# First attention of a three-part transformer kernel: the query root on GpSimd, a negated minimum for the softmax, an earlier exp table, reordered last additions

## The reference

```python
q = rmsnorm_2(q.reshape(B, S, A_HEADS, A_HEAD_DIM), q_gain)
k = rmsnorm_2(k.reshape(B, S, A_KV_HEADS, A_HEAD_DIM), k_gain)
...
scores = jnp.einsum('bnqkgd,bnskd->bnkgqs', q, kb).astype(jnp.float32) * scale   # scale = 1/8
bias = rel_bias[t5_bucket(dist)]
scores = scores + bias
scores = jnp.where(valid[None, :, None, None], scores, NEG)
m = jnp.maximum(jnp.max(scores, axis=-1, keepdims=True), sink)
p = jnp.exp(scores - m)
denom = jnp.sum(p, axis=-1, keepdims=True) + jnp.exp(sink - m)
probs = (p / denom).astype(v.dtype)
o = jnp.einsum('bnkgqs,bnskd->bnqkgd', probs, vb)
return o.reshape(B, S, A_HEADS * A_HEAD_DIM) @ w_out
```

## Time and profile before

| what | value |
|---|---|
| median of 3 runs (lowest, highest) | 2815.04 us (2812.4, 2815.44) |
| the profiled execution's own time | 2825.3 us |
| its span in the trace | 2824.1 us |
| PE busy | 2717.6 us (96%) |
| DVE busy | 1470.3 us (52%) |
| ACT busy | 974.7 us (35%) |
| POOL busy | 313.2 us (11%) |
| mean granted TensorE clock | 0.976 |

### The profile page before, as it was taken

One profiled execution on the slowest core, in us unless ns is written; L12 is line 12 of the kernel. 1 busy time (PEld: TensorE's weight loads), 2 busy tenths in 40 slices (PEclk: granted clock), 3 DMA queues, 4 the chain that ended last, 5 costly groups with the idle time before them and its releaser, 6 DMA issues.

```text
span 2824.1 us, 32255 instructions
## 1 busy us (share of the span) xinstructions
PE 2717.6 (96%) x13207; PEld 2278.7 (81%) x13207; DVE 1470.3 (52%) x2347; ACT 974.7 (35%) x1601; POOL 313.2 (11%) x381
## 2 busy tenths in 40 slices
PE   6899999999998999998999999999999888999999
PEld 5788788888786888888878888888888778888887
DVE  4635546665657545556665343544434466544433
ACT  3334333333353212234453222322223466432221
POOL 2000000000021000003340000000000467400000
PEclk9999999999999999998999999999999889999999
DMA  4322233623132287746223333232322100132331
GB/s 137 103 92 75 75 105 128 196 79 109 55 115 75 90 104 90 105 84 120 76 65 105 105 98 96 90 105 91 98 94 84 38 31 31 60 119 90 95 96 64
DMA packets 281195, 258.99 MB, mean 92 GB/s; under 512 B 40517, under 2 KB 276056, under 8 KB 281048
## 3 DMA queue, kind: packets, MB, share of 16 engines
q1 hardware_dynamic: 281047, 256.93, 33.1%
HBM read 242.23 MB, written 14.68 MB: 91 GB/s over the span
## 4 chain that ended last, share of the span: by engine, by line
PE 84%; DVE 9%; ACT 4%; issue 1%; SPq 1%; POOL 1%; DMA 1%; DVEq 0%; ACTq 0%; POOLq 0%
PE bank L1058 27%; PE bank L1059 26%; PE bank L1060 26%; DVE Wl L1730 1%; PE bank L1201 1%; PE bank L1069 1%; ACT Wh L1395 1%; SPq L2421 1%; PE bank L1343 1%; DVE Pl L1718 1%; DVE TMP L1923 1%; DVE TMP L1920 1%; DVE TMP L1799 0%; ACT TMP L1508 0%; DMA RAW<-in_a_w_in 0%
## 5 line engine op out<-in xcount | busy, mean ns | idle before, releaser
L1058 PE MATMUL bank<-Hh,Wl 128*128 128x512 f32 x2144 | 845.9, 395 | 15.1 <-DVE Hl L1746 15.1
L1059 PE MATMUL bank<-Hl,Wh 128*128 128x512 f32 x2144 | 838.7, 391 | 0.0
L1060 PE MATMUL bank<-Hh,Wh 128*128 128x512 f32 x2144 | 838.5, 391 | 0.0
L1395 ACT ACTIVATE Wh<-RAW 128x1024 fp32r<-128x1024 f32 (+2 forms) x454 | 441.0, 1023 | 440.6 <-PE bank L1060 378.3
L1730 DVE TENSOR_TENSOR Wl<-RAW,Wh 128x1024 fp32r<-128x1024 f32 (+2 forms) x420 | 492.7, 1216 | 172.2 <-ACT Wh L1395 171.7
L1058 PEld LDWEIGHTS bank<-Hh,Wl 128*128 128x128 f32 x2144 | 404.7, 189 | 103.9 <-issue 8.2
L1058 PE MATMUL bank<-Ph,Wl 128*128 128x512 f32 x1200 | 474.5, 395 | 13.2 <-DVE Pl L1812 3.5
L1060 PEld LDWEIGHTS bank<-Hh,Wh 128*128 128x128 f32 x2144 | 404.5, 189 | 86.3
L1059 PEld LDWEIGHTS bank<-Hl,Wh 128*128 128x128 f32 x2144 | 404.7, 189 | 84.9 <-issue 1.7
L1059 PE MATMUL bank<-Pl,Wh 128*128 128x512 f32 x1200 | 470.6, 392 | 0.0
L1060 PE MATMUL bank<-Ph,Wh 128*128 128x512 f32 x1200 | 470.4, 392 | 0.0
(11 more groups left out here) (296 smaller groups left out, 2506.4 us busy)
## 6 DMA issues: line engine op xcount, KB each, us to landing
RAW<-in_ffn_wg SPq DMA_DIRECT2D x44, 1024.0 KB, 5.3
RAW<-in_ffn_wu SPq DMA_DIRECT2D x44, 1024.0 KB, 5.3
RAW<-in_ffn_wd SPq DMA_DIRECT2D x32, 1024.0 KB, 5.2
RAW<-in_w_up SPq DMA_DIRECT2D x22, 1024.0 KB, 5.1
RAW<-in_w_in SPq DMA_DIRECT2D x20, 1024.0 KB, 5.1
RAW<-in_ffn_wd SPq DMA_DIRECT2D x16, 768.0 KB, 4.4
bias_scratch<-M SPq DMA_DIRECT2D x16, 512.0 KB, 8.0
RAW<-in_w_down SPq DMA_DIRECT2D x8, 1024.0 KB, 5.9
```

Source lines behind the costliest of these rows:

```text
L1058: mm(o, ll, rh, start=start, stop=False)
L1059: mm(o, lh, rl, start=False, stop=False)
L1060: return mm(o, lh, rh, start=False, stop=stop)
L1395: run(Wh[:, n % 3, x:y], RAW[:, n % 2, x:y], ACT.Copy).then_inc(*w_hi.up(("w_hi", n, i)))
```

## The change

Four things change, all in the first attention.

1. **Query root.** VectorE's twelve instructions become two on GpSimd: add 64 times 1e-6 to the sum of squares, then the power -0.5 (`rms`, `rq`). The result is one eighth of the former root, so the score's factor 1/8 is in it, and the key's gain is used without the factor (`gk_a8` goes). VectorE's part of `a_q_norm` keeps a wait and the scaling of `qt`. `a_q_out` of a group's first block gets a wait for the addition of the group before.
2. **Softmax.** The bias step writes the negated sum and takes the minimum with the negated sink, so the sixteen negations (line 2078) go. The exp gets a scale of -1 and waits for each half of a head's scores by itself. One instruction of 128x16 that negates the sinks takes the place of the one that made `gk_a8`.
3. **Exp table.** An exp of 128x1 after the second half of the values (`a_kv`) makes ScalarE load the table there and not at the first head.
4. **Last additions.** In the last pass the pair and the sum of squares of column c-1 come behind the addition of column c; those of column 7 come last.

```diff
-            if j == 3:
+            for x in [c - 1] * (j == 3 and c > 0) + [c] * (j == 3 and c == 7):
                 if after:
-                    after(c)
-                if c < late:
-                    sums(c)
+                    after(x)
+                if x < late:
+                    sums(x)
...
@@ ScalarE @@
                 ins.then_inc(*pair_hi.up(("a_v_hi", half)))
+                if half:
+                    run(sm[:, 13:14], mhalf, ACT.Exp)
...
-                act.wait_ge(*at(("a_nmax", h)))
                 for n, (z0, z1) in enumerate(SEG):
-                    run(S[:, z0:z1], S[:, z0:z1], ACT.Exp, bias=nm[:, n:n + 1], accum_out=sums_[:, n:n + 1])
+                    if n % 2 == 0:
+                        act.wait_ge(*at(("a_biased", h, n // 2)))
+                    run(S[:, z0:z1], S[:, z0:z1], ACT.Exp, bias=nm[:, n:n + 1], scale=-1.0, accum_out=sums_[:, n:n + 1])
...
@@ VectorE @@
-                ts(gk_a8, gk_a, 0.125, None, ALU.mult).then_inc(*dve_out.up("a_gain"))
-                dve.wait_ge(*at("a_gain"))
+                ts(nsink, sinkc, -1.0, None, ALU.mult).then_inc(*dve_out.up("a_sinks"))
...
                 dve.wait_ge(*at(("a_qsq", g, b)))
+                if g and b == 0:
+                    dve.wait_ge(*at(("a_qss_in", g - 1)))
...
                 g, = s
-                dve.wait_ge(*at(("a_qss", g, 3)))
-                rsqrt(rq, ssq, 64, ("a_rq", g))
                 dve.wait_ge(*at(("a_rq", g)))
...
-                        ins = dve.e.tensor_tensor_reduce(S[:, z0:z1], o[:, z0 - c0:z1 - c0], B[:, z0:z1], 1.0,
-                                                         sinkc[:, h:h + 1], ALU.add, ALU.max, mx[:, n:n + 1])
+                        ins = dve.e.tensor_tensor_reduce(S[:, z0:z1], o[:, z0 - c0:z1 - c0], B[:, z0:z1], -1.0,
+                                                         nsink[:, h:h + 1], ALU.add, ALU.min, nm[:, n:n + 1])
                     ins.then_inc(*dve_out.up(("a_biased", h, m), free=("a_s", h, m)))
-                dve.wait_ge(*at(("a_biased", h, 1)))
-                ts(nm, mx, -1.0, None, ALU.mult).then_inc(*dve_out.up(("a_nmax", h)))
...
@@ GpSimd @@
+            elif kind == "a_q_norm":
+                g, = s
+                pool.wait_ge(*at(("a_qss", g, 3)))
+                if g:
+                    pool.wait_ge(*at(("a_rq", g - 1)))
+                tt(rms, ssq, eps64.broadcast_to([128, 16]), ALU.add).then_inc(*pool_out.up(("a_qss_in", g)))
+                pool.wait_ge(*at(("a_qss_in", g)))
+                if g:
+                    pool.wait_ge(*at(("a_qn", g - 1)))
+                tt(rq, rms, mhalf.broadcast_to([128, 16]), ALU.pow).then_inc(*pool_out.up(("a_rq", g)))
```

More of the change, by code:

```diff
@@ L914, in build @@
     lo = sm[:, 9:10]
-    mhalf, most = sm[:, 11:12], sm[:, 12:13]
+    mhalf, most, eps64 = sm[:, 11:12], sm[:, 12:13], sm[:, 14:15]
     rinv = sm[:, 16:32]
@@ L1002, in build @@
           (Ph[:, 2, :], Pl[:, 2, :])]
-    gk_a8 = sm[:, 10:11]
+    nsink = small[:, 48:64]
     ssk, rk = small[:, 0:8], small[:, 8:16]
     rk4 = rk.rearrange("p (n g) -> p n g", n=4)
-    ssq, rq = small[:, 16:32], small[:, 32:48]
+    ssq, rq, rms = small[:, 16:32], small[:, 32:48], small[:, 64:80]
     def pflat(W, a, b):
@@ L1564, in act_program @@
                 act.wait_ge(*at(("a_kt", g)))
-                run(Ph[:, g, :], bank(("a_kt", g)), ACT.Copy, scale=gk_a8).then_inc(*pair_hi.up(("a_kT_hi", g)))
+                run(Ph[:, g, :], bank(("a_kt", g)), ACT.Copy, scale=gk_a).then_inc(*pair_hi.up(("a_kT_hi", g)))
             elif kind == "a_q_turn":
@@ L2051, in dve_program @@
                 dve.wait_ge(*at(("a_kT_hi", g)))
-                stt(Pl[:, g, :], bank(("a_kt", g)), gk_a8, f(Ph[:, g, :]), ALU.mult, ALU.subtract).then_inc(
+                stt(Pl[:, g, :], bank(("a_kt", g)), gk_a, f(Ph[:, g, :]), ALU.mult, ALU.subtract).then_inc(
                     *pair_lo.up(("a_kT", g), free=("a_kt", g)))
@@ L2063, in dve_program @@
                 S, B, x = SS[h % 3], BR[h % 2], 16 * (h % 4)
-                mx, nm = sm[:, 160 + x:164 + x], sm[:, 164 + x:168 + x]
+                nm = sm[:, 164 + x:168 + x]
+                dve.wait_ge(*at("a_sinks"))
                 for m in range(2):
@@ L2216, in pool_program @@
                 memset(mhalf, -0.5)
+                memset(eps64, 64 * EPS)
                 memset(most, -LOWEST)
```

## The result

| | before | after |
|---|---|---|
| median, first comparison (4 runs each) | 2815.24 us (2812.4 to 2820.12) | 2799.59 us (2794.0 to 2800.02) |
| ratio, 95% interval | | 0.9938 [0.9919, 0.9957] |
| median, second comparison (15 and 5 runs) | 2817.39 us (2810.84 to 2822.08) | 2794.82 us (2794.43 to 2800.01) |
| ratio, 95% interval | | 0.9925 [0.9910, 0.9939] |
| profiled execution: own time, span | 2825.3, 2824.1 us | 2799.72, 2798.5 us |

The change makes the kernel faster by 15.6 us in the first comparison and 22.6 us in the second. The second comparison was run later; before it 16 to 20 us were expected of the medians, and more came.

What follows compares the result with a forecast made beforehand. TensorE, busy 96% of the span, was taken as the bound, with about 17 us of waits and 14 us of clock to gain in the first attention. 1.2 + 2.5 + 2.7 + 1.5 + 1.0 + 3.9 = 12.8 us gave 2802.2 us, range 2796 to 2807.

Steps and rivals of the forecast that it cites:

- rival A: VectorE's scaling starts ahead of GpSimd's weight tile in the first attention: 23.8 us gained, 2791.2 us; chance 0.20.
- The root's own terms: First attention, query groups 0 to 3: gains of 1.2, 2.5, 6.6 and 1.5 us, 11.8 us in all.
- the tail: Last additions at the end of the first attention: forecast 1.0 us, bounds 0 to 3.0 us.
- The root's length: Query root on GpSimd: addition 0.30 us from start to start, then power 2.91 us, 3.2 us in all.
- Who goes first: Behind the power in groups 0 to 2: GpSimd's weight tile starts first, VectorE's scaling waits for one half, 2.4 us.
- Group 0: Ahead of its turns: scaling ends at 1307.3 against 1308.48, 1.2 us gained, 2.6 us wait left, no clock back.
- Group 1: Ahead of its turns: scaling ends at 1333.3 against 1335.81, 2.5 us gained, clock left as it is.
- Group 2 and 3: Group 2: all 2.7 us of wait and 3.9 us of clock go; group 3: the 1.47 us wait goes, 1.5 us.
- Last additions: Last pass of the first attention: a column takes 2.0 instead of 2.15 us, 1.0 us over seven columns.
- Nothing for negations and table: Softmax and exp table: sixteen negations (3 us together) go and the table load (1.28 us) moves, bringing nothing.
- B: VectorE's scaling waits for the whole weight tile: 3.2 us gained, 2811.8 us, no change that can be told; chance 0.12.
- C: Clock stays at 0.50 for 10 us longer at each of three places: 6 us slower, 2821 us; chance 0.05.

## Why the prediction was right in part

**The sum.** 12.8 us were forecast for the stage, some 22 were found. The time came out near by luck, because the first comparison of medians showed 15.6 us; the second, with 22.6, is nearer to what the stage says, and nearer to rival A's 23.8, though what A describes did not happen. The waits were too small by 3 to 4 us (8.9 of 11.5 to 12.5), most of it at the end and in group 1; the clock was too small by 6.5 to 7 (3.9 of 10.4 to 10.8), because it also came back behind group 1 and at the end. The root's own terms were near: 11.8 us forecast, 12.2 to 14.8 with the root alone.

Two sums in the prediction are off by themselves. The waits that it lists make 18.1 us, not "about 17", and it leaves out 0.71 us behind the turns of group 0. With the tail at 3.0 us and all clock terms the lower end is 2794.5 us, not 2796. Neither touches the forecast.

**The root's length: right.** Four powers of 2.91 us, 3.2 us from the start of the addition.

**Who goes first: right in two groups of three.** In groups 0 and 1 the scaling lasted 3.41 us (forecast 3.6). In group 2 it lasted 1.23 us: the tile's high part came 0.27 us after the power, so VectorE was first. The prediction had the high part at 1362.97 and the root's end at 1363.1, 0.13 us the other way, too close to decide. It cost nothing: the scaling ended 3.9 us before TensorE turned (1358.56). Timelines of POOL and DVE in after, group 2:

```profile
1350.51 2.91 POOL L2282 TENSOR_TENSOR sm<-sm 128x16 f32<-128x16 f32 x1
1353.68 5.59 POOL L2239 TENSOR_TENSOR Wl<-RAW,Wh 128x1024 fp32r<-128x1024 f32 x2 [0.27 <-ACT Wh L1395]
...
1353.45 1.23 DVE L2050 TENSOR_TENSOR M<-M,sm 128x1024 f32<-128x1024 f32 x1
```

**Group 0: the term right, the remaining wait wrong.** Forecast 1.2 us, with 2.6 us left; 1.12 us was left. The step that failed is the start. The sums were taken to be ready 4.2 us ahead of TensorE, as in the one trace read; in the other traces it is 4.9 to 5.6 us. Against the usual wait of 2.41 us the gain is 1.3.

**Group 1: too small.** Forecast 2.5 of the 4.06 us; 3.8 went. The step "the exp's waits by halves start it up to a microsecond earlier, off the path" failed: the scaling of head 1, and behind it the power, stand behind that exp in GpSimd's list. The root alone leaves 1.33 us, so the root's own term was right (2.7 us). And the clock, left "as it is", came back in both traces of after.

**Group 2 and 3: right** (6.6 for 5.0 to 6.1, and 1.5 for 1.8).

**Last additions: 1.0 us for 5.9 to 7.0.** The step that failed is "a column still takes 2.0 us; over seven columns": beside GpSimd's additions it takes 1.71 us, and the first two of the seven take 1.36 us. The upper bound named there, 3.0 us and 3.2 of clock, is what came.

**Nothing for negations and table: right alone** (0.9999 [0.9990, 1.0008]), wrong together with the root by 0.8 to 1.0 us of waiting. Whether the clock behind group 1 belongs to it is open.

**The rivals.** A (VectorE first) happened in group 2 alone, where it was worth nothing; made on purpose in all groups, it gave 3.3 us in the stage. B (the whole tile) did not happen. C (clock stays low) did not: in both traces of after the clock was 1.00 behind groups 1 and 2, and fell once, for 6.8 us, behind group 0.

## What to carry to other kernels

Ask of an engine that gets new work what its list waits for, not only what the work costs: a chain that was off the path (the exp) lies on it as soon as a root stands behind it on the same engine. Put a consumer's short instruction ahead of a long one of another engine that would hold it up, by a wait of one semaphore; here GpSimd stood idle for 1.3 us, where nobody needed it, VectorE's scaling became 2.2 us shorter, and TensorE waited 1.1 us less in group 0. And before a sum is made from one profiled execution, compare its own time with the median: where it is 10 us off, the stage of interest should be read in a second trace.

## What the runs showed of the hardware

- The lower clock does not follow from the length of the wait before it alone. The stretches (PE waits ahead of and behind the turns, then the time at 0.50): 1.12 and 1.13 us, 6.8 us; 1.13 alone in group 0, 3.4 us; 1.33 and 1.65 us in group 1, 3.4 us; 0.29 and 1.65 in both traces of after, none, but 0.31 and 1.65 without GpSimd's additions at the end, 3.4 us; 1.75 alone, none. So a low stretch of 3.4 us comes and goes with the same waits, and one trace can't put it down to a change. Windows of after behind groups 0, 1 and 2:

```profile
1308.60:1315.40 6.80, 6.80 (x32) 6.58 (x32) 2.83 (x13) 3.01 (x12) 1.83 (x2) 0.50 0.68 224
1331.44:1341.44 10.00, 10.00 (x82) 9.79 (x83) 7.38 (x26) 6.02 (x22) 3.38 (x4) 1.00 0.60 196
1361.35:1371.35 10.00, 10.00 (x70) 9.08 (x71) 4.17 (x15) 5.05 (x14) 6.53 (x4) 1.00 0.36 136
```

- The clock moves the time of unchanged code by more than many changes do: the second attention took from 192.6 to 200.1 us in fourteen traces, with 29.7 to 33.0 us of waiting.
- A VectorE instruction of 128x4 was held up as well: behind a weight tile in group 1 of after, the softmax's sum (line 2085) lasted 2.31 us instead of 0.16.
